# Last mixer of a two-model block kernel: the down projection, latent norms and up projections put into one program line

## The reference, cut to what matters

```python
def mla_down(h, w_down):
    return jnp.split(h @ w_down, [MLA_Q_RANK, MLA_Q_RANK + MLA_KV_RANK], axis=-1)   # 384, 256, rope 64

def mla_q(q_a, q_norm, w_uq, rope):
    q = (rmsnorm(q_a, q_norm) @ w_uq).reshape(B, L, MLA_HEADS, MLA_NOPE + MLA_ROPE)  # 8 heads, 128 + 64
    q_n, q_r = jnp.split(q, [MLA_NOPE], axis=-1)
    return jnp.concatenate([q_n, apply_rope2d(q_r, *rope)], axis=-1)

def mla_kv(kv_a, k_r, kv_norm, w_ukv, rope):
    kv = (rmsnorm(kv_a, kv_norm) @ w_ukv).reshape(B, L, MLA_HEADS, MLA_NOPE + MLA_V)
    ...

def attend(q, k, v):
    s = jnp.einsum('bqhd,bkhd->bhqk', q, k).astype(F32) * MLA_SCALE       # 192 ** -0.5
    p = jax.nn.softmax(s, axis=-1).astype(v.dtype)
    return jnp.einsum('bhqk,bkhd->bqhd', p, v)
```

## Time and profile before

| | us |
|---|---|
| median of 3 runs | 3291.71 |
| lowest and highest run | 3284.9, 3295.43 |
| span of the profiled execution | 3283.7 |
| PE busy in that span | 3050.2 (93%) |
| DVE busy | 1899.8 (58%) |
| ACT busy | 1119.9 (34%) |
| POOL busy | 90.5 (3%) |

### The profile page before, as it was taken

The page is one execution under the profiler, slowest core; times in us unless marked ns, Lnnn a source line. Parts: engine busy times, 40 slices in busy tenths (PEclk is TensorE's granted clock), DMA queues, the critical chain, the costliest instruction groups (busy, mean ns, idle before and its releaser), DMA issues. The chain is left out here.

```text
span 3283.7 us, 39921 instructions
## 1 busy us (share of the span) xinstructions
PE 3050.2 (93%) x16274; PEld 2693.9 (82%) x16274; DVE 1899.8 (58%) x2841; ACT 1119.9 (34%) x1658; POOL 90.5 (3%) x74
## 2 busy tenths in 40 slices
PE   7988999999879999999967789999999889999998
PEld 5767888887768888899946389999999867689997
DVE  5754775856555878765546664542553355456464
ACT  4443422235344222433335123221222245333232
POOL 0031000000130000000000000000000000000000
PEclk9998999999999999999978889999999989999999
DMA  3100554521103556412100121121122110123222
GB/s 127 50 28 20 174 176 143 191 86 52 46 7 109 194 173 193 140 58 103 58 7 1 56 82 53 65 66 57 65 64 65 69 56 8 61 85 98 91 93 87
DMA packets 73136, 275.78 MB, mean 84 GB/s; under 512 B 7835, under 2 KB 11419, under 8 KB 71804
## 3 DMA queue, kind: packets, MB, share of 16 engines
q1 hardware_dynamic: 72956, 273.25, 25.1%
HBM read 264.83 MB, written 8.39 MB: 83 GB/s over the span
## 5 line engine op out<-in xcount | busy, mean ns | idle before, releaser
L122 PE MATMUL banks<-normed_hi,weights_hi 128*128 128x384 f32 (+2 forms) x2672 | 887.9, 338 | 11.5 <-DVE normed_lo L1030 11.5
L123 PE MATMUL banks<-normed_lo,weights_hi 128*128 128x384 f32 (+2 forms) x2672 | 885.1, 337 | 0.0
L104 ACT ACTIVATE weights_hi<-weights_raw 128x1024 fp32r<-128x1024 f32 (+3 forms) x365 | 395.6, 1084 | 1244.0 <-PE banks L125 1218.7
L125 PE MATMUL banks<-normed_hi,weights_lo 128*128 128x384 f32 (+2 forms) x2672 | 742.9, 338 | 0.0
L110 DVE TENSOR_TENSOR weights_lo<-weights_raw,weights_hi 128x1024 fp32r<-128x1024 f32 (+3 forms) x365 | 459.9, 1260 | 138.0 <-ACT weights_hi L104 134.5
L122 PEld LDWEIGHTS banks<-normed_hi,weights_hi 128*128 128x128 f32 x2672 | 504.1, 189 | 39.8 <-DVE normed_lo L1030 12.2
L123 PEld LDWEIGHTS banks<-normed_lo,weights_hi 128*128 128x128 f32 x2672 | 506.3, 189 | 27.3
L125 PEld LDWEIGHTS banks<-normed_hi,weights_lo 128*128 128x128 f32 x2672 | 473.4, 190 | 27.4
L123 PE MATMUL banks<-hidden_lo,weights_hi 128*128 128x512 f32 (+1 forms) x880 | 323.0, 367 | 0.0
L122 PE MATMUL banks<-hidden_hi,weights_hi 128*128 128x512 f32 (+1 forms) x880 | 323.0, 367 | 0.0
L125 PE MATMUL banks<-hidden_hi,weights_lo 128*128 128x512 f32 (+1 forms) x880 | 294.7, 367 | 0.0
(11 more groups left out here) (424 smaller groups left out, 4248.1 us busy)
## 6 DMA issues: line engine op xcount, KB each, us to landing
weights_raw<-in_w_up SPq DMA_DIRECT2D x176, 512.0 KB, 3.4
ada_tiles<-in_ada SPq DMA_DIRECT2D x96, 512.0 KB, 3.5
weights_raw<-in_w_down SPq DMA_DIRECT2D x64, 704.0 KB, 4.0
weights_raw<-in_w_in SPq DMA_DIRECT2D x67, 512.0 KB, 3.4
weights_raw<-in_w_out SPq DMA_DIRECT2D x32, 512.0 KB, 3.4
x_kept<-x SPq DMA_DIRECT2D x2, 3072.0 KB, 10.5
x<-x_kept SPq DMA_DIRECT2D x1, 3072.0 KB, 10.0
weights_raw<-in_mla_down SPq DMA_DIRECT2D x6, 512.0 KB, 3.4
```

The source lines that it names most:

```text
L104: act.activation(self.hi[:, n % 2, 0:w], self.raw[:, n % 2, 0:w], ACT.Copy).then_inc(self.high_ready, 1)
L122: pe.matmul(out, self.hi[:, s, m], xh, start=k == 0, stop=False)
L123: pe.matmul(out, self.hi[:, s, m], xl, start=False, stop=False)
L125: mm = pe.matmul(out, self.lo[:, s, m], xh, start=False, stop=k == kt - 1)
```

## The change

The five blocks of `mla` go. The down projection's Line goes on with the up projections; what the norms did happens beside the down projection's tiles, in a helper `Latents` that `Shifted` calls:

- The tiles of the down projection come in another order: 2 of the values' and keys' latents, 3 of the queries', 1 of rope keys (written straight into its buffer, with no copy).
- Values and keys: squares of both tiles on ACT; 24 instructions of column sums on PE at the start of tile 3 (24, as each product of fp32 takes two); root, reciprocal; spread over the partitions on PE at tile 3, k 6; copied by ACT into a buffer; scaling by DVE; high and low parts.
- Queries: the latents are only multiplied with the norm's weight and split; their 1/rms isn't applied to them. Their squares' column sums (24 instructions) stand at tile 5, k 6; root and reciprocal give one column for each 128 queries, times 192 ** -0.5.
- Attention takes that column as its scale, in L1429 and in the exponential (L1467), where it had a number.
- The load of w_v is issued behind the down projection's own loads and waits for its first product, since it lands where the feed-forward's hidden tiles were. The buffers of attention are put at fixed places.
- ACT waits, before it writes the first high part of the keys, until the store of x has ended (the keys lie over x).

```diff
 class Shifted(Stage):
@@ tensor, before(j), at(k)
+                if self.latents:
+                    self.latents.tensor(pe, j, k)
@@ scalar, after the tile is written
+            if self.latents:
+                self.latents.scalar(act, j)
@@ vector, after the low part of the weights of tile j + 2
+            if self.latents:
+                self.latents.vector(dve, j)
 class Plain(Stage):
@@ tensor
-            Z.R.products(pe, self.first + j, Z.outs(self.t0 + j, self.form), self.rhs)
+            Z.R.products(pe, self.first + j, Z.outs(self.t0 + j, self.form), self.rhs,
+                         (lambda k: self.after(pe, k)) if self.after and j == 0 else None)
+class Latents:
+    KV, Q = 2, 3
+    def q_ready(self, pe, k):
+        pe.wait_ge(self.Z.mix["q_lo"], k + 1)
+    def sums(self, pe, tiles, n):
+        for t in range(n):
+            for i, x in enumerate(tiles):
+                mm = pe.matmul(self.Z.spread_ps[:, 0, t:t + 1], x[:, t * P:(t + 1) * P], self.Z.K["ones"][:, 0:1],
+                               start=i == 0, stop=i == len(tiles) - 1)
+        mm.then_inc(self.Z.mix["latent_sums"], 1)
+    def tensor(self, pe, j, k):
+        Z, on = self.Z, self.Z.mix
+        if (j, k) == (3, 0):
+            pe.wait_ge(Z.scale_ready, self.norm.m + 1)
+            pe.wait_ge(on["latent_squared"], self.KV)
+            self.sums(pe, self.squares[:self.KV], TOK // P)
+        if (j, k) == (3, 6):
+            pe.wait_ge(on["latent_inverted"], 1)
...
+                    mm = pe.matmul(Z.spread_ps[:, n, m * P:(m + 1) * P], self.kv_cols[:, t:t + 1].broadcast_to([P, P]),
+                                   Z.K["ident"], start=True, stop=True)
+            mm.then_inc(on["latent_spread"], 1)
+        if (j, k) == (5, 6):
+            pe.wait_ge(on["latent_rows"], 1)
+            pe.wait_ge(on["latent_squared"], self.KV + self.Q)
+            self.sums(pe, self.squares[self.KV:], LT)
+    def scalar(self, act, j):
+        if j < self.KV + self.Q:
+            act.wait_ge(Z.drained, self.out0 + j + 1)
+            if j >= self.KV:
+                n = j - self.KV
+                act.activation(self.q[0][:, n], self.tokens(j), ACT.Copy,
+                               scale=self.q_gain[:, n:n + 1]).then_inc(on["q_hi"], 1)
+            act.activation(self.squares[j], self.tokens(j), ACT.Square).then_inc(on["latent_squared"], 1)
+        if j == 2:
+            act.wait_ge(on["latent_sums"], 1)
+            act.activation(self.kv_cols, ..., ACT.Sqrt, ...).then_inc(on["latent_root"], 1)
+        if j == 3:
+            act.wait_ge(on["latent_spread"], 1)
...
+        if j == 4:
+            for n in range(self.KV):
+                act.wait_ge(on["kv_scaled"], n + 1)
+                act.activation(self.kv[0][:, n], self.raw[:, n], ACT.Copy).then_inc(on["kv_hi"], 1)
+        if j == 5:
+            act.wait_ge(on["latent_sums"], 2)
+            act.activation(self.q_cols, ..., ACT.Sqrt, ...).then_inc(on["latent_root"], 1)
+    def vector(self, dve, j):
...
+        if j == 5:
+            dve.wait_ge(on["latent_root"], 2)
+            dve.reciprocal(self.q_cols, self.q_cols).then_inc(on["latent_inverted"], 1)
+            dve.wait_ge(on["latent_inverted"], 2)
+            dve.tensor_scalar(self.q_cols, self.q_cols, 192 ** -0.5, None, ALU.mult).then_inc(on["latent_inverted"], 1)
 class ValueWeights(Stage):
     def sync(self, sp):
+        sp.wait_ge(self.Z.R.product, self.after)
         sp.dma_start(self.w[:], self.source).then_inc(self.Z.mix["values_in"], 16)
 def attention(...)
-                    dve.tensor_scalar(s[:, 1:2], s[:, 0:1], -scale, None, ALU.mult).then_inc(max_ready, 1)
+                    dve.tensor_scalar(s[:, 1:2], s[:, 0:1], scale[:, n % 4:n % 4 + 1], -1.0, ALU.mult,
+                                      ALU.mult).then_inc(max_ready, 1)
-                    act.activation(dst, src, ACT.Exp, bias=sm[:, n % 2, 1:2], scale=scale,
+                    act.activation(dst, src, ACT.Exp, bias=sm[:, n % 2, 1:2], scale=scale[:, n % 4:n % 4 + 1],
                                    accum_out=sm[:, n % 2, 2:3]).then_inc(exp_done, 1)
 def build(...)
-        with ExitStack() as mx:
-            Hm = mx.enter_context(split_pair(nc, "mixed", KT, SEQ))
-            mla(nc, K, R, c, down, Hm, X, ins)
+        attend = Mla(Z, nc, K, c, ins)
...
         Z.run(mixed, up_shifts, *ffn, Keep(Z, X, kept, lambda sp: ffn[-1].done(sp, KT - 1)),
-              ShiftsThere(down_shifts), Shifted(Z, kinds, H2, Norm(Z, SEGS, ffn[-1].added), ffn[-1].h0), Await(Z))
+              ShiftsThere(down_shifts), down, *attend.stages(Z, ins, down), Await(Z))
+        attend.attend()
-    a["mla_down"] = tiled(np.concatenate([w, w[:, 640:704]], axis=1))
+    a["mla_down"] = tiled(np.concatenate([w[:, 384:640], w[:, :384], w[:, 640:704], w[:, 640:704]], axis=1))
```

More of the change, by code:

```diff
@@ L190, in form_of @@
     return Form(segs, [(0, SEQ)], 0)
[L193 to L238, removed]
@@ L897, with __init__ @@
 class Shifted(Stage):
-    def __init__(self, Z, kinds, H, norm, h_base, taps=None, bias=None, held=0, twice=None, keep=None):
+    def __init__(self, Z, kinds, H, norm, h_base, taps=None, bias=None, held=0, twice=None, keep=None, latents=None):
         self.Z, self.kinds, self.H, self.norm, self.h_base, self.taps, self.bias = Z, kinds, H, norm, h_base, taps, bias
-        self.held, self.twice, self.keep = held, twice, keep
+        self.held, self.twice, self.keep, self.latents = held, twice, keep, latents
         self.first, self.t0 = Z.take_tiles(len(kinds))
@@ L911, in __init__ @@
         self.col = Z.buffer("shift_cols", [P, 2, 2], Z.col_at)
+        if latents:
+            latents.begin(norm, self.out0)
     def sync(self, sp):
@@ L1197, with __init__ @@
 class Plain(Stage):
-    def __init__(self, Z, tiles, rhs, form, high, low, rest=None, paired=None, also=None):
-        self.also = also
+    def __init__(self, Z, tiles, rhs, form, high, low, rest=None, paired=None, also=None, after=None, home=None):
+        self.also, self.after, self.home = also, after, home
         self.Z, self.n, self.rhs, self.form = Z, tiles, rhs, form
@@ L1254, with __init__ @@
 class ValueWeights(Stage):
-    def __init__(self, Z, w, high, low, source):
-        self.Z, self.w, self.high, self.low, self.source = Z, w, high, low, source
+    def __init__(self, Z, w, high, low, source, after):
+        self.Z, self.w, self.high, self.low, self.source, self.after = Z, w, high, low, source, after
     def sync(self, sp):
+        sp.wait_ge(self.Z.R.product, self.after)
         sp.dma_start(self.w[:], self.source).then_inc(self.Z.mix["values_in"], 16)
@@ L1347, in vector, with attention @@
         low(4)
-def attention(nc, K, heads, keys, scale, score_parts, values, vrows, out):
+def attention(nc, K, heads, keys, scale, score_parts, values, vrows, out, probs_at, turned_at):
     kt = keys // P
@@ L1496, in _ @@
                     dve.tensor_copy(out, ps[:, n % 2, 0:len(ins)]).then_inc(copied, 1)
-def copy_tiles(nc, pairs):
-    with stage(nc, "copied") as (block, copied):
-        @block.vector
-        def _(dve):
-            for dst, src in pairs:
-                dve.tensor_copy(dst, src)
 def weave(*strands):
```

263 lines of the change are left out of this document (113 added, 150 removed).

## The result

| | us, median (lowest to highest, runs) | ratio to before on the same chip [95%] |
|---|---|---|
| first measurement: before | 3288.68 (3284.9 to 3295.43, 4) | |
| first measurement: after | 3257.1 (3256.09 to 3260.54, 4) | 0.9911 [0.9893, 0.9929] |
| second measurement, another chip: before | 3281.55 (3279.07 to 3296.07, 23) | |
| second: after | 3260.34 (3254.91 to 3262.59, 6) | 0.9929 [0.9915, 0.9943] |
| third, another chip: before | 3281.82 (3280.14 to 3292.47, 11) | |

The change makes the kernel faster, as forecast. The predicted 3267.8 us is 10.7 above the 3257.1 measured, and the range, 3260 to 3276, doesn't hold it: that prediction was wrong. The second pair of rows, with most runs of before, gives 3281.55 * (1 - 0.9929) = 23.3 us gained, where the sum said 23.9.

The account below looks back on a forecast made before the run. PE, busy for 93% of the span, was taken as the bound. The terms, -31.9 - 1.7 - 0.2 + 6.5 + 3.2 + 0.2 = -23.9 us, from a median of 3291.7 gave 3267.8 us, range 3260 to 3276.

Parts of the forecast that it names:

- the base of the sum: Whole kernel: before's median of 3291.7 us, 8.0 above the profiled span of 3283.7, from which the saving was subtracted.
- The hole, -31.9: Between down projection and first query matmul: PE's wait through norms and barriers goes, 31.9 us removed.
- The clock comes back, -1.7: First query tile: its 9 matmuls take 2.05 us at full clock instead of 3.77, 1.7 us removed.
- The third query tile, -0.2: Third query tile's start: a stall of 0.7 us for late weights shrinks to 0.5, 0.2 us removed.
- What PE gets, +6.5: PE in the down projection: two column sums of 24 matmuls, 5.2 us, and one spread, 1.3 us, added.
- The clock behind such sums, +3.2: Behind both new column sums in the down projection: PE's granted clock falls, 1.6 us lost each, 3.2 added.
- rival A: Down projection: the clock doesn't fall behind the sums, or behind one only; -27.1 us, 3264.6 us; chance 0.25.
- ACT and DVE, 0: Down projection tiles: the norm steps fit in ACT's and DVE's idle time, so PE never waits; cost 0.
- rival C: Down projection: a norm step is late and PE waits 20 us or more; 3283 to 3292 us; chance 0.04.
- Attention, +0.2: Attention: scale columns lengthen DVE's and ACT's instructions, but PE's loop hides them; only filling it costs 0.2 us.
- B: Attention: the cover is gone and the column's price shows each unit, +1.9 to +5.1 us; chance 0.15.
- D: Attention: PE pauses each unit and its clock falls, 23.4 us lost at 0.83, making it slower; chance 0.03.

Follow-up runs that it names:

- before_again: The kernel before, unchanged, run and traced again: 3283.53 us, ratio 1.0001 to the other runs of the same kernel.
- before_columns: The kernel before with attention's scale as a column instead of a number, nothing else changed: 3284.09 us, ratio 1.0005 to before.
- after_again: The changed kernel, unchanged, run again for a second trace: 3260.34 us, ratio 0.9929 to before.
- after_third: The changed kernel, unchanged, run once more on another chip for a third trace: 3262.47 us, ratio 0.9932 to before.
- after_cut: The changed kernel with its line cut behind the down projection, so one barrier stands again ahead of the queries: 3264.87 us, ratio 0.9945 to before.

## Why the prediction was wrong, point by point

**The step that failed is the base of the sum**: "The span stands 8.0 below the median of the runs shown, for what lies around it". What lies around a span is 1.7 to 1.9 us in each of the ten profiled executions whose own time is known. The other 6.2 were scatter: before's profiled execution took some 3283.7 + 1.8 = 3285.5 us (the fourth run of the first measurement, 3285.65, fits it), and the median of the three runs shown happened to lie high, at 3291.7, where 23 runs on the next chip lie from 3279 to 3296 with their median at 3281.55. From 3285.5 the sum gives 3261.6, and 6.2 of the miss of 10.7 are gone. That the median of the three was high, and not the first chip slower, rests on that chip's four runs alone.

**The rest of the miss**, 3261.6 - 3257.1 = 4.5 us, comes apart by the ruler in the two first traces. The spans differ by 29.4, not 23.9: 6.0 from where the store of x stands (identical code, and before_again has 2553.9 too: chance), 26.4 from the mixer, less 2.9 that after takes longer from the reload to the end (434.7 and 437.6; before_columns has 437.5 as well). So 6.0 - 2.9 = 3.1 lie outside the mixer, where the code is the same, and 26.4 - 23.9 = 2.5 are errors of terms; the median of after then lies 1.0 above its profiled run.

**The range** failed with it. It allowed for "what three runs scatter", about 4 us. Twenty-three runs of the same kernel on one chip lie 17 us apart, and in three measurements after's median was 3257.1, 3260.34 and 3262.47: two of the three inside the range. That the last two came inside is luck of the same kind. A median of few runs cannot be forecast to 8 us on either side when both it and the one it starts from move like this.

The terms, in the prediction's order:

- *The hole, -31.9*: right, to within 0.1 (2613.30 to 2613.65, as 2611.10 to 2611.45 was assumed).
- *The clock comes back, -1.7*: right (2.07 us for 9 matmuls, 2.05 forecast).
- *The third query tile, -0.2*: stall 0.3 and not 0.5, so -0.4. ACT is late as described: its root for the queries starts at 2616.00, only behind the last down tile's L800. In the first trace there was also a wait of 0.8 at 2638.09, and none of the kind in after_again, where the query and value tiles up to the first score matmul took 70.6 us and not 71.7.
- *What PE gets, +6.5*: right (2.59, 2.60, 1.26 us and a start 0.1 late). By the Trainium skill's floor of about 25 ns (TensorE: Matmul & The Clock Gate, "Wait — 56ns, not 53.3ns?") both sums would take an estimated 1.2 us; this trace has 0.108 from start to start, and the measurement decides. Each of these matmuls also has a weight load of its own here (24 of them, 2.82 us of PEld).
- *The clock behind such sums, +3.2*: oversized. It fell behind the first sums only, in all three traces of after: +1.6. That is rival A's "behind one only", which the prediction priced like no fall at all (-27.1); with one fall the sum is -25.5, and from 3285.5 that gives 3260.0. The row that the term rests on was itself a matter of luck: behind the same 20 matmuls the clock fell in three of the eleven traces, before, after_again and after_third. The 4 us behind them in before and in before_again (columns as in the earlier trace rows):

```profile
1414.70:1418.70 4.00, 4.00 (x16) 4.00 (x16) 2.09 (x6) 1.51 (x3) 0.00 (x0) 0.57 0.00 0
...
1413.20:1417.20 4.00, 4.00 (x25) 4.00 (x25) 2.08 (x6) 1.51 (x3) 0.00 (x0) 1.00 0.00 0
```

- *ACT and DVE, 0*: right. No PE wait at tiles 3 and 5; rival C falls.
- *Attention, +0.2*: right that the loop hides the columns; its score groups took 112.8 us in both traces of after, against 113.2 and 112.8 before. B and D fall: the clock in attention is 1.00.
- *Not in the sum*: from the last score group to the reload after took 15.6 us, before 17.1. The granted clock there is 0.89 in one and 0.80 in the other; after_again has 0.79 and takes 16.6. It moves from run to run, as does the start of attention.

The 2.5 are what is left of errors both ways. By pieces of the stretch, in the two first traces: to the first query matmul 23.7 us gained, forecast 22.2 (the clock); from there to the first score matmul 0.7 (72.4 and 71.7), forecast 1.9 (after has the wait of 0.8, and PE's pause ahead of attention is 4.95 against 4.44); over the score groups 0.4, forecast 0.2 lost; from the last of them to the reload 1.5, forecast none. The second pair of traces has 23.6, 2.7, 0.0 and 0.5. Only the first piece repeats; that the errors of the other three (1.2 one way, 2.1 the other) largely cancel is luck.

## What to carry to other kernels

Make a sum of differences against one execution, but take the forecast's base from the scatter of as many runs as there are, and measure what lies around a span instead of reading it off as span against median. Cut both traces at two points that the change doesn't touch: 26.4 us in that stretch were repeatable to 0.4, when the whole program moved by 17. Where steps of a norm move under a matmul stage, one-column matmuls are the price on PE; let an idle engine add the tiles first (28 matmuls fewer, 3.0 us here), and put that addition ahead of what nobody waits for. Before a single trace's clock becomes a term, look for the same place in other traces.

## What the runs showed of the hardware

- The granted clock falls to half behind, or inside, one-column matmuls although PE never idles. 24 in a row: behind the first sums in three of the four traces that have them with this line or the cut one, behind the second in none. 48 in a row: both times, from within the sums, for 10.2 us. The 20 at 1412.54 of before, which all eleven traces have: in three of them. 12 in a row, the down projection's own sums: in none of the eleven; the 12, 8, 6 and 4 of the experiments: in none of their traces, one or two each. Why the same matmuls show it in one execution and not in the next, and why the second 24 never do, stays open.
- The same instructions ahead of the mixer take 403.6 to 406.0 us or 413.2 to 413.4, by whether PE is granted half clock for some 7 or 31 us in one place. With 9.8 us it is more than half of the 17 us over which 23 runs scatter.
- From the reload to the end all versions with after's line take 437.5 or 437.6 us, after_cut takes 434.7; before takes 434.7 and 434.5, and before_columns 437.5. So the 3 us don't go with the change. In all eight traces with 437.5 or 437.6 PE's granted clock is 0.55 to 0.58 for 3.8 us just behind the reload (2814.90 to 2818.70 in after: 12 matmuls), and 1.00 in the three with 434.5 to 434.7 (2830.20 to 2834.00 in after_cut: 19). Seven matmuls at 0.23 us are 1.6 of the 3 us; the rest was not looked for.
